# Sliding-window attention: the order of take-outs, exponentials and scalings on ScalarE and VectorE

## What is computed

```python
def one_block(args):          # n: a block of 128 queries, all 16 heads
    s = jnp.einsum('bqhgd,bkhd->bhgqk', qb, kb) + bias      # keys of two blocks
    s = jnp.where(valid, s, -1e30)
    m = jnp.maximum(jnp.max(s, axis=-1, keepdims=True), sink)
    p = jnp.exp(s - m)
    denom = jnp.sum(p, axis=-1, keepdims=True) + jnp.exp(sink - m)
    p = (p / denom)
    return jnp.einsum('bhgqk,bkhd->bqhgd', p, vb)
...
return o @ w_o + b_o
```

## Time and profile before

| | us |
|---|---|
| median of 3 runs | 1422.33 (1418.08 to 1423.3) |
| profiled execution | 1416.9 |
| its span | 1415.0 |
| PE busy | 1259.5 (89%) |
| VectorE busy | 410.2 (29%) |
| ScalarE busy | 325.6 (23%) |
| GpSimd busy | 153.7 (11%) |
| chain that ended last | PE 63%, DMA 26%, DVE 7%, ACT 2% |

### The profile page before, as it was taken

How to read it: one execution, slowest core, us unless ns; L and a number is a source line. 1 busy time by engine, 2 the same in 40 slices (tenths; PEclk the granted TensorE clock), 3 DMA queues, 4 the chain that set the end, 5 groups by cost and what they waited for, 6 DMA issues and landing times.

```text
span 1415.0 us, 15354 instructions
## 1 busy us (share of the span) xinstructions
PE 1259.5 (89%) x6042; PEld 672.2 (48%) x6042; DVE 410.2 (29%) x871; ACT 325.6 (23%) x620; POOL 153.7 (11%) x125
## 2 busy tenths in 40 slices
PE   5978798999999999988389998999999999998891
PEld 4756564444443433333168886744444434333330
DVE  6454453112111111111445454321112111111114
ACT  3235542211211112111331121112122111211112
POOL 5650030000000000000000000201000000000000
PEclk8989999999999999999679999999999999999996
DMA  9200635999999999999922232399999999999995
GB/s 351 86 0 1 244 150 240 427 428 426 429 428 428 429 426 429 428 427 427 340 44 89 89 119 119 125 427 426 428 426 428 429 428 427 429 427 427 428 422 212
DMA packets 63859, 456.17 MB, mean 322 GB/s; under 512 B 14852, under 2 KB 30238, under 8 KB 39236
## 3 DMA queue, kind: packets, MB, share of 16 engines
q1 hardware_dynamic: 52436, 444.29, 75.4%
q0 software_dynamic: 5120, 8.41, 1.6%
q10 hardware_dynamic: 6256, 2.80, 0.8%
HBM read 444.96 MB, written 18.90 MB: 328 GB/s over the span
## 4 chain that ended last, share of the span: by engine, by line
PE 63%; DMA 26%; DVE 7%; ACT 2%; issue 1%; POOLq 0%; DVEq 0%; ACTq 0%
PE ps L833 20%; PE ps L1063 20%; PE ps L1081 11%; DMA xt<-in_moe_w_gate_up_dram 10%; DMA big<-in_moe_w_gate_up_dram 10%; PE ps L1040 6%; DMA xt<-in_moe_w_down_dram 5%; PE ps L1053 1%; DVE xr L1201 1%; PE ps L1072 1%; PE ps L974 1%; PE ps L1048 1%; PE ps L914 1%; PE ps L819 1%; PE ps L881 1%
## 5 line engine op out<-in xcount | busy, mean ns | idle before, releaser
L1063 PE MATMUL ps<-big,arena 128*64 128x512 f32 x1024 | 228.1, 594 | 21.4 <-DMA big<-in_moe_w_gate_up_dram 20.7
L1452 DVE TENSOR_TENSOR gain<-arena,ps 64x512 f32<-64x512 f32 x64 | 68.7, 1073 | 432.9 <-ACT arena L721 432.9
L528 POOL DMA_INDIRECT rows<-arena x64 | 62.5, 977 | 880.6 <-DVE arena L1478 880.6
L721 ACT ACTIVATE arena<-ps 64x512 f32<-64x512 f32 x64 | 37.7, 590 | 518.7 <-PE ps L1063 518.7
L1063 PEld LDWEIGHTS ps<-big,arena 128*64 128x64 f32 x1024 | 72.3, 137 | 171.5 <-issue 136.2
L1063 PE MATMUL ps<-small,arena 128*64 128x512 f32 x512 | 114.9, 594 | 10.6 <-DMA small<-in_moe_w_gate_up_dram 10.6
L833 PE MATMUL ps<-xt_parts,small_parts 128*128 128x512 f32 x288 | 113.9, 405 | 6.9 <-DVE big L1260 5.4
L1081 PE MATMUL ps<-big,arena 128*64 128x512 f32 x512 | 116.9, 598 | 0.0
L833 PE MATMUL ps<-xr_parts,small_parts 128*128 128x512 f32 x272 | 108.5, 399 | 0.0
L833 PE MATMUL ps<-xt_parts,big_parts 128*128 128x512 f32 x256 | 101.6, 397 | 0.0
L1040 PE MATMUL ps<-arena_parts 128*128 128x512 f32 x256 | 83.6, 408 | 3.1 <-DVE arena_parts L1448 3.1
(11 more groups left out here) (169 smaller groups left out, 1518.5 us busy)
## 6 DMA issues: line engine op xcount, KB each, us to landing
big<-in_moe_w_gate_up_dram SPq DMA_DIRECT2D x64, 2048.0 KB, 29.0
small<-in_moe_w_gate_up_dram SPq DMA_DIRECT2D x32, 2048.0 KB, 29.6
big<-in_moe_w_down_dram SPq DMA_DIRECT2D x32, 2048.0 KB, 32.8
xt<-in_moe_w_gate_up_dram SPq DMA_DIRECT2D x16, 2048.0 KB, 29.8
arena<-in_moe_w_gate_up_dram SPq DMA_DIRECT2D x16, 2048.0 KB, 30.1
small<-in_moe_w_down_dram SPq DMA_DIRECT2D x16, 2048.0 KB, 32.8
arena<-in_moe_w_down_dram SPq DMA_DIRECT2D x8, 2048.0 KB, 32.7
xt<-in_moe_w_down_dram SPq DMA_DIRECT2D x8, 2048.0 KB, 34.7
```

Source lines behind the costliest of these rows:

```text
L528: nc.gpsimd.indirect_dma_start(out=rows_dram[l], out_offset=bass.IndirectOffsetOnAxis(ap=where[:, j:j + 1], axis=0), in_=y_rows[:, j, :], ...
L721: nc.scalar.activation(silu[BLOCK:P, j, :], ps[2 + j][0:BLOCK, :], ACT.Silu).then_inc(S.silu_ready, 1)
L1063: mm = nc.tensor.matmul(ps[2 + j][half * BLOCK:(half + 1) * BLOCK, :], xg[:, k, j * BLOCK:(j + 1) * BLOCK], w[:, a, half * FF:(half + 1) * ...
L1452: V.tensor_tensor(hid[BLOCK:P, j, :].rearrange("q (k p) -> q p k", p=P), silu[BLOCK:P, j, :].rearrange("q (p k) -> q p k", p=P), ps[2 + j] ...
```

## The change

ScalarE's and VectorE's calls in attention are put in another order, and three helpers get an argument for it. In round u:

- both engines take out unit u-1 before anything else (ScalarE: before the exponentials of u+1 and the scaling of u; VectorE: before the bias of u+2);
- ScalarE then does the first four exponentials of u+1, copies banks f = 0, 1, the other four exponentials, copies f = 2, 3, and last scales its half of u+1 (before: all exponentials of u+1, its half of u, take-out, four copies). The scaling of unit 0 comes before the loop;
- in unit 7 `root(1, 0)` stands between the two pairs of copies; `root(1, 1)` comes before the last take-out, as does `norm_tile(1, 1)` on VectorE;
- VectorE does the scaling of unit 1 in two parts, around `take_queries(6)`;
- the squares of `root`, whose values nobody reads, go to the place of the keys in every layer, since the place used before (`x_high`, where the transposed probabilities lie in attention) is now still being written when `root(1, 0)` runs.

PE, GpSimd and SyncE keep their programs. Line numbers in the changed kernel are 1 to 10 higher (L653 becomes L654, L1309 becomes L1318).

```diff
-                nc.scalar.activation(x_high[:, t] if i % 2 else squares_at, h[:, t, :], ACT.Square,
+                nc.scalar.activation(squares_at, h[:, t, :], ACT.Square,
...
-            def att_exp(u):
+            def att_exp(u, half):
                 b = u % 3
-                act.wait_ge(peak_ready, u + 1)
                 hi = P if unit(u)[0] == 0 else 2 * P
-                nc.scalar.activation(sink_e[:, b, :], sink_e[:, b, :], ACT.Exp).then_inc(sink_ready, 1)
-                for k in range(HG):
+                if half == 0:
+                    act.wait_ge(peak_ready, u + 1)
+                    nc.scalar.activation(sink_e[:, b, :], sink_e[:, b, :], ACT.Exp).then_inc(sink_ready, 1)
+                for k in range(half * HG // 2, (half + 1) * HG // 2):
...
-            def att_turn(u):
-                for f in range(4):
+            def att_turn(u, fs):
+                for f in fs:
                     act.wait_ge(pT_ps, 4 * u + f + 1)
...
-            att_exp(0)
+            att_exp(0, 0)
+            att_exp(0, 1)
+            att_scale(0)
             for u in range(U):
-                if u + 1 < U:
-                    att_exp(u + 1)
-                att_scale(u)
                 if u >= 1:
                     att_take_out(u - 1)
-                if u == U - 1:
+                if u + 1 < U:
+                    att_exp(u + 1, 0)
+                att_turn(u, (0, 1))
+                if u + 1 < U:
+                    att_exp(u + 1, 1)
+                else:
                     root(1, 0)
-                att_turn(u)
+                att_turn(u, (2, 3))
+                if u + 1 < U:
+                    att_scale(u + 1)
+            root(1, 1)
             att_take_out(U - 1)
-            for t in range(1, TT):
+            take_turned(1, 0)
+            for t in range(2, TT):
                 root(1, t)
                 take_turned(1, t - 1)
...
 
-            def att_scale(u):
+            def att_scale(u, halves):
 
                 b = u % 3
                 hi = P if unit(u)[0] == 0 else 2 * P
                 dve.wait_ge(sink_ready, u + 1)
...
             att_bias(1)
             take_queries(4, ps[7])
-            att_scale(0)
+            att_scale(0, (0, 1))
             att_bias(2)
             take_queries(5, ps[7])
+            att_scale(1, (0,))
             take_queries(6, ps[7])
-            att_scale(1)
+            att_scale(1, (1,))
             take_queries(7, ps[7])
             dve.wait_ge(h_biased, TT)
             for u in range(1, U):
                 g, t = divmod(u - 1, TT)
+                att_take_out(u - 1)
                 if u + 2 < U:
                     att_bias(u + 2)
-                att_take_out(u - 1)
                 add_heads(g, t, 0)
                 if u + 1 < U:
-                    att_scale(u + 1)
+                    att_scale(u + 1, (0, 1))
                 else:
                     norm_tile(1, 0)
                 add_heads(g, t, 1)
+            norm_tile(1, 1)
             att_take_out(U - 1)
-            norm_tile(1, 1)
             take_turned(1, 0)
             add_heads(1, TT - 1, 0)
             norm_tile(1, 2)
```

More of the change, by code:

```diff
@@ L1293, in att_scale @@
                 dve.wait_ge(sink_ready, u + 1)
-                for half in range(2):
+                for half in halves:
                     heads = slice(half * 4, half * 4 + 4)
```

## The result

| | before | changed kernel |
|---|---|---|
| first comparison, median | 1420.20 (4 runs, 1417.94 to 1423.3) | 1398.11 (4 runs, 1395.85 to 1400.5) |
| ratio, 95% interval | | 0.9843 [0.9811, 0.9876] |
| second comparison | 1418.86 (17 runs) | 1400.90 (5 runs), 0.9871 [0.9853, 0.989] |
| third comparison | 1418.20 (9 runs) | 1400.55 (5 runs), 0.9868 [0.9851, 0.9885] |
| profiled execution, its span | 1416.9, 1415.0 | 1400.2, 1398.4 |

The kernel became faster: by 22.1 us in the first comparison, 18.0 and 17.7 in the two others, where 17.9 was forecast. The first median, 1398.11, lies 6.3 us under the forecast of 1404.4 and at the very edge of the range (1398): 2.1 us of that is the median of before, which fell from 1422.33 to 1420.2 when a fourth run came in, and 4.2 us the gain itself.

A forecast was written before the change was run, and what follows sets the result against it. PE's 16.5 us of waits for take-outs in attention were taken to delay the expert stream; 15.0 - 0.55 + 2.95 - 0.5 + 0.97 = 17.9 us off the median 1422.33 gave 1404.4 us, range 1398 to 1411.

The forecast's parts named there:

- take-out goes first: Attention, PE's wait ahead of projections: gone in units 1 to 5, 0.5 us left three times; 15.0 us gained.
- added heads later, unit 1: Attention, unit 1: the first half of heads is added at about 105.8, so PE waits 0.55 us; -0.55.
- clock in units 1 and 6: First projections of units 1 and 6: back at 2.4 GHz time, 1.36 + 1.59 = 2.95 us gained; bounds nothing or all.
- end of attention: Last projection: take-out later behind the second norm, -0.5 us; PE's wait for that norm gone, +0.97 us.
- What bounds the kernel: Expert weight stream starts only after attention and routing, so ending attention earlier moves everything behind it by the same time.
- The bias comes later: VectorE in attention: bias later by the take-out, 0.7 us; added heads covered by 0.2 us, except in unit 1.
- thin cover of 0.2 us: Ahead of the second projection: added heads ready at 6.45, wanted by PE at 6.7.
- the rival that put 0.8 us on each of five units: Units 1 to 5: added heads come 1 us later, PE waits 4 us more in all, time 1408; chance 0.14.
- Exponentials in halves: ScalarE in attention: exponentials start only after the take-out and scaling comes last; no effect on time.
- a sign of being wrong: Attention: table loads between 100 and 175 us would show the prediction wrong.
- The rival with a load at each change: ScalarE's round: four table loads of 1283 ns make it 15.3 us, 6.5 us slower, 1429; chance 0.04.
- The range: Whole kernel's time: 1398 to 1411 us for 8 in 10.

The follow-up runs named there:

- whole_exp: The changed kernel with all eight exponentials in one piece ahead of the four copies; median 1398.0 us, ratio 0.9855 to the kernel before.
- old_end: The changed kernel with the last take-out ahead of `root(1, 1)` and `norm_tile(1, 1)`, as before the change; median 1400.05 us.
- scalar_only: The changed kernel with VectorE's loop and both engines' ends in the old order, so only ScalarE's new order stays; median 1415.88 us.
- before_again: The kernel before, traced a second time with nothing edited; one run, profiled at 1421.27 us.
- before_third: The kernel before, traced a third time with nothing edited; one run, profiled at 1415.79 us.
- vector_only: The kernel before with only VectorE's take-out moved ahead of the bias, ScalarE keeping its old order; median 1404.75 us.
- no_filler: The changed kernel without the two filler products ahead of the last transposes, `turn_tile(1, 3)`, in routing; median 1401.23 us.

## Why the prediction was right or wrong, step by step

The mechanism was right: the take-outs were what PE waited for, and the gain came where it was forecast. What failed are the sizes of two terms of the sum, and a term that it lacked. PE's steps from start to start, in the traces of before and after, give:

| term of the sum | forecast | measured |
|---|---|---|
| take-out goes first | 15.0 | 16.3 |
| added heads later, unit 1 | -0.55 | -0.6 |
| clock in units 1 and 6 | 2.95 | 2.96 |
| end of attention | -0.5 + 0.97 | 1.10 |
| attention together | 17.9 | 19.8 |
| clock in routing | no term | -1.7, in the third trace -4.5 |

Of the 4.2 us by which the gain of the first comparison exceeds the forecast, attention explains 1.9. The cause of the other 2.3 stays open: two of its four executions, at 1395.85 and 1396.01, were not traced.

- **What bounds the kernel** was right. The first gate product came 18.2 us earlier (18 forecast), slice 8 by the same 18.2, and the rest of the program stayed at 1187.4 to 1189.9 us in all fourteen traces. The 1.5 us that the first pair of traces lost there was 0.4 when the changed kernel was traced again (1187.8 against 1187.4) and 1.3 in its third trace. Single traces differ there by up to 2.5 us, and whether a part of that goes with the change is not shown.
- **The take-out goes first** was right as a mechanism and shown by the two halves: VectorE's order alone gives 16.1 us, ScalarE's alone 2.9. The left-over wait of 0.5 us, three times, was 0.49, 0.49 and 0.65. The size, 15.0 us, was too small. I had added up idle times that are counted from modelled ends of matmuls. Starts are surer: in unit 5 PE's step from the transposes to the projection went from 3.52 to 0.84 us, 2.68, where the row gives 2.43 of idle, since a projection without a wait starts 0.25 us before the modelled end (1.09 us) of the transposes. The same holds in units 1 to 5, where the wait is gone (4.31, 2.07, 2.71, 3.15 and 2.68 us), and not in unit 6, where one is left (1.34). Together 16.3 us.
- **The bias comes later:** the wait of 0.55 us in unit 1 was there with 0.51. The chain of waits of the changed kernel has it, between the small steps and the projection:

```profile
102.76 1.82 DVE arena L1294
...
104.90 0.69 DVE h L1326
105.59 0.04 issue
105.64 3.03 PE ps L842 x12
```

  The small step's end did not move, as the prediction said. The other wait for added heads, 0.35 us in unit 4 (138.52 above), is the one of before (151.63; it is the 0.3 of the earlier trace rows), so the change brought no second one. The thin cover of 0.2 us held in units 2, 3 and 5, and the rival that put 0.8 us on each of five units is out.
- **The clock in units 1 and 6** was right. The first projection of unit 1, in PE's timeline of the changed kernel:

```profile
101.25 0.48 PE L842 MATMUL ps<-small_parts,xt_parts 128*128 128x512 f32 x1
...
104.09 1.03 PE L910 MATMUL ps<-ident,arena 128*128 128x128 f32 x8
```

  Its twelve products take 2.84 us from start to start, where before took 4.19; in unit 6 it is 2.81 and 4.42. That is 1.35 + 1.61 = 2.96 us, and PEclk is 1.00 from 98 to 163.5 us. That all of it came back was a choice between two bounds, nothing or all, and it held in each of the changed kernel's three traces.
- **Exponentials in halves:** nothing of it is on the path, as forecast, and no table load stands between exponentials and copies. The one load in attention is that of the first square root, in both kernels: 184.55 before, 166.84 after, which is inside the stretch where the prediction would have read a load as a sign of being wrong. The rival with a load at each change is out: `ACT 325.9` against 325.6 us leaves no room for one more load of 1283 ns. What the prediction did not price is what the halves are for: 1.4 us (`whole_exp`), 0.9 of it in the unit without scores.
- **The end:** forecast -0.5 + 0.97, measured -0.16 + 1.26, 1.10 in all (`old_end`). The norm began 0.97 us before `att_out(7)` ended, as the sum had it (9.2 against 10.1), but the take-out was late by 0.16 us and not 0.5. The sum added durations end to end; on the chip the norm took 2.04 and the take-out behind it began at 175.07, 0.17 us before the norm's end. On the norm's length the trace agrees with the Trainium skill (SBUF — State Buffer, "SBUF: two separate sides"): the norm came first and kept its 2.04 us, and GpSimd's copy, which came second, took 1.70 instead of 1.03.
- **Left out: what the clock does in routing.** No term of the sum looked behind attention. The traces of the changed kernel lost 1.7, 1.7 and 4.5 us there against the 27.05 of before. That is about as much as attention gave beyond the forecast (1.9), or more, and of the other sign, so it is luck that the medians of the later comparisons (18.0 and 17.7 us) meet the forecast of 17.9: two errors cancel.
- **The range** was drawn around one median of before with 3 us of spread. Its lower end is about the profiled execution of before less 17.9 (1399.0), so it had room for a fast execution of before but none for a gain above 17.9. Over all comparisons the changed kernel ran 14 times with a median of 1400.5 (1395.85 to 1402.33), before 43 times with 1418.6 (1415.5 to 1425.6).

What stays open: whether it is the denser attention that makes PE's clock fall in routing. For it: three of three traces of the changed kernel against one of three of before. Against it: these are few, one trace of before fell as far (0.88), and `scalar_only`, whose attention is only 2.9 us shorter, had a mean granted clock of 0.94 and a routing of 28.63 us, while `whole_exp`, with an attention almost as dense as the changed kernel's, had the same 0.94 and 27.26 us. And the executions of 1395.85 and 1396.01 us have no trace; that the clock was up in their routing is not shown.

## What to carry to other kernels

When a producer has a long job that nobody waits for yet (the bias, two units ahead) and a short one that the busiest engine is about to ask for (the take-out), the short one goes first on every engine that takes part: here one engine's order alone gave 16 of 20 us, the other's 3. Count what a wait costs from start to start, not from the idle time beside a modelled end, and look at the stage behind the one that gets shorter before adding its gain to the total. Where medians scatter by several microseconds, judge a part of one microsecond by its stage in the trace.

## What was not expected of the hardware

Executions of one kernel scatter by several microseconds, and the granted clock accounts for a part of that. In the traces it can be followed: `before_again` and `before_third` differ by 5.5 us, of which 4.8 lie in attention and routing, both with a lower PEclk in the slower one.

The mean granted clock of a whole execution tells less. Of the kernel before, those with at least 0.968 took 1415.5 to 1419.0 us (17 runs), those with at most 0.963 took 1420.2 to 1425.6 (10 runs), but the twelve between, at 0.964 to 0.966, took anything from 1416.9 to 1423.4. Of the changed kernel, three with 0.970 and 0.971 took 1395.85, 1396.01 and 1397.17, ten with 0.964 to 0.967 took 1399.52 to 1402.33; one with 0.969 took 1400.5. And the six executions of `vector_only` all had 0.969 or 0.970 and took 1398.07 to 1405.01, in two groups 6 us apart. So the scatter can't be taken out of a median by this number, and that the gain would be the whole 19.8 us of attention with an equal clock in routing is not shown.

The clock does not follow the longest wait. In attention of the kernel before, unit 5 waited 2.43 us and unit 4 had a wait of the same kind, and both projections ran at 2.4 GHz (2.99 us in unit 4), while units 1 and 6 fell to 1.2 GHz for a while the earlier trace rows. Units 2 and 6 had the same idle time ahead of their projections, 1.82 us, and only unit 6 fell. Units 1 and 6 fell in all three traces of before; unit 3 fell in `before_again` alone (15.68 us instead of 14.11). In routing it fell with waits of 0.88 us between logits of 40 columns (`no_filler`, 0.72 over 30.7 us), and adding or removing 1.7 us of filler products changed no median by more than the scatter.
